# A gated conv and pooling trunk on eight cores: first-tile work in pieces, tanh gates, PSUM banks by last use

## The chip, the cores and the metric

One Trainium2 chip, all 8 cores. Each core runs the same program on one of the 8 prompt sequences and on 16 of the 128 sample sequences; the cores exchange nothing. The metric is the device time of the slowest core in microseconds.

## The reference

With `x` of 2048 tokens x 1024 channels (prompt) or 4 tokens x 1024 for each sample sequence, and six modulation vectors from `silu(c) @ w_ada + b_ada`:

```
h  = rms(x) * (1 + sc1) + sh1
z  = h @ w_in                       # a_val, a_gate, u, ga, gb, 1024 columns each
a  = a_val * sigmoid(a_gate)
cn = layernorm(depthwise_conv31(a) + conv_b)
o_a = silu(cn) @ w_conv_out
pooled = trailing_mean(u, window 2, 4, 8 or 16 by channel group) - u
o_b = (pooled @ pool_mix per group * pool_scale) @ w_pool_out
m  = sigmoid(ga) * o_a + sigmoid(gb) * o_b
x  = x + g1 * (m @ w_out)
x  = x + g2 * (relu(h2 @ w_ff1)^2 @ w_ff2)   # h2 = rms(x) * (1 + sc2) + sh2
y  = rms(x) * final_g
```

The last 30 rows of `a` and the last 15 of `u` are outputs too.

## The kernel before, in words

**Tiles.** Channels lie on the 128 partitions in 8 chunks `j`. The prompt is cut into 4 tiles of 512 tokens; the 64 sample tokens ride along with tile 0 (and with the MLP of tile 0) as extra matmuls of 64 columns. A stage is a loop over `j`: 8 matmuls 128x128x512 into one PSUM bank, then an eviction. The stages of a tile are A (the GLU, two groups a `j`), U (pooling input), G with index 0 and 1 (the two gates), PO and CO (the two branch outputs), O (output projection). The MLP, stage F, of tile t-1 stands between A and U of tile t.

**Weights.** They come in blocks of 1 MB of bf16 into 5 ring slots, in an order written out in `plan`. `use_block` takes the next block and issues loads up to 5 ahead (4 while a merge runs); each load goes into the slot that the block before has just left. A first load reads f32 and casts, from the POOL queue (L332); each block is saved once to a scratch in DRAM (L341, SP) and later read from there (L329, SP). In tile 0 the 12 blocks of `w_ada` stand between the others: `mod_half` (L491 on) turns one into half of a modulation vector. POOL runs its queue in order, so a load that waits for TensorE to leave a slot holds what is behind it.

**Tile 0.** All 31 conv taps run on TensorE as diagonal matrices (`conv0(p)`, two chunks a call, L738 on), with the sample's taps beside them (L717); diagonals are built two groups ahead by ScalarE (L697) and POOL (L700). `conv0` stands behind A `j` = 3, 5 and 7 and behind U `j` = 3. The sample history `shist` goes to `xT[1]` in one load (L1168), 8·16·34 bf16 elements a partition (1.1 MB), issued ahead of stage A; `pmT` and `uhist` (1344 f32 elements a partition, 0.69 MB) follow on SP (L1180, L1181). `s_pool` (L552 on) does the sample's pooling: 20 adds on POOL (L568) and 8 final operations on VectorE (L574). `merge_po` (L983 on) multiplies `pool_mix` into one half of `w_pool_out`: 8 chunks of 2 matmuls, evicted in turn by ScalarE (L993) and VectorE (L996), all in one piece ahead of PO `j` = 0 and 4.

**Later tiles.** 8 of the 31 taps run on TensorE, 23 on VectorE (L773), spread by a credit count (`pump`) over A, F, U and G0; `drain` finishes them ahead of `ln`.

**Small chains.** `rms_stats`, `s_rms` and `ln` sum squares by TensorE (L480, L526) into a PSUM bank, take a root on ScalarE, a reciprocal and a diagonal on VectorE (L465), and spread the result by a matmul with a matrix of ones (`bcast`, L474). They are generators; `hooks((j, step(g)), ...)` runs one step of `g` behind chunk `j` of a stage. `norm3` (final norm of the tile before, 8 VectorE operations at L671 that read its bank) stands in U, G0 `j` = 7 and G1 `j` = 0 to 2; `ln` (statistics, then 8 chunks by VectorE L809, POOL L811 and ScalarE Silu L813) in G1 `j` = 2, 6, 7 and PO 0 to 5; `norm1` of the next tile in PO, CO and O. ScalarE evicts gates with a Sigmoid (L971). VectorE multiplies them in at L1015 and L1035.

**PSUM.** `get_ps` hands out 4 general banks in turn, skipping held ones; `unhold`, at the point where the last reader is *issued*, puts a held bank back into the turn. The other 4 banks are for the conv.

```
i = rr["gen"]
while GEN[i] in held:
    i = (i + 1) % len(GEN)
rr["gen"] = (i + 1) % len(GEN)
```

Dependences are found by buffer (`Sched.op`): a reader waits for the last writer issued before it, a writer for the last writer and all readers. Each engine takes its instructions strictly in the order of the program.

## Time and profile before

| what | value |
|---|---|
| median of 3 runs | 1327.47 us (1325.97 to 1329.53) |
| the profiled execution, its own time | 1327.52 us |
| its span on the slowest core (core 0) | 1325.9 us |
| spans of the 8 cores | 1316.9 to 1325.9 us |
| mean granted TensorE clock by core | 0.940 to 0.943 |
| TensorE busy | 1138.7 us (86%) |
| VectorE, ScalarE, POOL busy | 50%, 41%, 35% |

How to read it: the span runs from the first instruction to the last on one core; 1.6 us of the time lie around it. Tile 0 takes the first 344 us (TensorE starts tile 1 at 344.1 us), three tiles with the MLP take about 270 us each, and the MLP of the last tile ends it. The granted clock is a share of 2.4 GHz; 0.5 is 1.2 GHz. A busy TensorE says nothing of its speed, so busy time and granted clock are read together.

### The profile page before, as it was taken

Reading aid. Unit: us, or ns where it says so; the run is one execution under the profiler, and the core shown is the slowest. Engines: PE = TensorE matmul, PEld = TensorE weight load, DVE = VectorE, ACT = ScalarE, POOL = GpSimd, SP = SyncE. Lnnn points to the kernel's source line nnn. Section 1 sums busy time; section 2 is a strip of 40 time slices with the busy share of each in tenths; the row PEclk is TensorE's granted clock in tenths of the full one; section 3 lists DMA queues with packets and bytes.
Section 4 is the critical chain, followed back from the end, with each engine's and each line's share of the span. In section 5 each row is a group of like instructions: output and inputs, shape, how many; then the busy total and the mean of one; then the engine's idle time right before and its main releaser. Section 6 shows DMA issues by size and latency. Waiting matters only on the chain.

```text
span 1325.9 us, 25435 instructions; the slowest of 8 cores (1316.9 to 1325.9 us)
## 1 busy us (share of the span) xinstructions
PE 1138.7 (86%) x6514; PEld 543.9 (41%) x6514; DVE 660.1 (50%) x1063; ACT 539.1 (41%) x970; POOL 469.0 (35%) x414
## 2 busy tenths in 40 slices
...
GB/s 170 211 166 65 101 71 170 188 95 221 162 136 141 166 146 172 151 221 193 128 164 190 155 191 227 164 213 131 124 195 174 186 181 127 162 128 96 159 96 64
DMA packets 40639, 205.52 MB, mean 155 GB/s; under 512 B 3968, under 2 KB 4352, under 8 KB 26496
## 3 DMA queue, kind: packets, MB, share of 16 engines
q0 software_dynamic: 20112, 76.62, 36.1%
q1 hardware_dynamic: 20384, 127.28, 28.3%
...
## 4 chain that ended last, share of the span: by engine, by line
PE 74%; DMA 6%; issue 5%; DVE 5%; ACT 4%; POOL 4%; POOLq 0%; DVEq 0%; SPq 0%; ACTq 0%
PE ps L383 47%; PE ps L1106 17%; PE ps L712 6%; DMA ring<-wblk 5%; PE ps L480 2%; PE ps L474 1%; POOL dgp L700 1%; DVE xT L671 1%; DMA xT<-xin 1%; POOL accN L447 1%; DVE tn L645 1%; POOL tn L811 1%; ACT tq L457 1%; POOL tp L888 1%; PE ps L717 1%
## 5 line engine op out<-in xcount | busy, mean ns | idle before, releaser
L773 DVE SCALAR_TENSOR_TENSOR ps<-aext,cw_sb,ps 128x512 f32<-128x512 bf16 x552 | 368.7, 749 | 5.2 <-PE ps L712 5.2
L383 PE MATMUL ps<-h,ring 128*128 128x512 bf16 x1280 | 303.7, 395 | 27.3 <-DMA ring<-wblk 22.7
L383 PE MATMUL ps<-s_t,ring 128*128 128x512 bf16 x1280 | 297.7, 389 | 14.1 <-ACT s_t L813 7.6
L1106 PE MATMUL ps<-r2f,ring 128*128 128x512 bf16 x1024 | 225.6, 382 | 5.1 <-ACT r2s L1095 5.1
L447 POOL TENSOR_TENSOR accN<-accN,tq 128x512 f32<-128x512 f32 x84 | 106.5, 1268 | 280.1 <-ACT tq L457 277.1
L383 PEld LDWEIGHTS ps<-h,ring 128*128 128x128 bf16 x1280 | 127.0, 102 | 184.9 <-issue 56.6
L383 PEld LDWEIGHTS ps<-s_t,ring 128*128 128x128 bf16 x1280 | 124.8, 100 | 168.3 <-issue 33.2
L332 POOL DMA_DIRECT2D ring<-wblk x72 | 52.9, 735 | 300.9 <-PE ps L383 178.8
L1106 PEld LDWEIGHTS ps<-r2f,ring 128*128 128x128 bf16 x1024 | 100.2, 98 | 125.9 <-issue 8.3
L457 ACT ACTIVATE tq<-xT 128x512 f32<-128x512 f32 x84 | 50.8, 624 | 215.8 <-DVE xT L1110 184.8
L383 PE MATMUL ps<-pooled,ring 128*128 128x512 bf16 x512 | 117.0, 383 | 11.6 <-DVE sgs L1044 4.1
L712 PE MATMUL ps<-aext,dgp 128*128 128x512 bf16 x440 | 109.1, 380 | 5.0 <-POOL dgp L700 5.0
L1082 ACT ACTIVATE ps<-ps 128x512 f32<-128x512 f32 x128 | 74.6, 583 | 92.5 <-PE ps L383 92.5
L1110 DVE SCALAR_TENSOR_TENSOR xT<-ps,modT,xT 128x512 f32<-128x512 f32 x32 | 24.0, 751 | 166.0 <-PE ps L1106 139.2
L700 POOL TENSOR_TENSOR dgp<-identb,cw_sb 128x1024 bf16<-128x1024 bf16 x36 | 67.8, 1893 | 85.9 <-PE ps L712 51.9
L1083 ACT ACTIVATE r2f<-ps 128x512 bf16<-128x512 f32 x128 | 76.4, 597 | 11.7
L383 PEld LDWEIGHTS ps<-pooled,ring 128*128 128x128 bf16 x512 | 48.8, 98 | 72.0 <-issue 17.7
L839 DVE TENSOR_TENSOR aext<-ps,tp 128x512 bf16<-128x512 f32 x32 | 22.1, 691 | 110.7 <-PE ps L383 96.3
L893 DVE SCALAR_TENSOR_TENSOR pooled<-tp,r2f 128x512 bf16<-128x512 f32 x32 | 36.2, 1138 | 77.3 <-POOL tp L888 48.0
L811 POOL TENSOR_TENSOR tn<-tn,bcs 128x512 f32<-128x512 f32 x32 | 40.1, 1265 | 85.1 <-DVE tn L809 85.1
L712 PEld LDWEIGHTS ps<-aext,dgp 128*128 128x128 bf16 x440 | 42.4, 97 | 59.0 <-issue 10.1
L971 ACT ACTIVATE r2f<-ps 128x512 f32<-128x512 f32 x64 | 36.6, 595 | 63.7 <-PE ps L383 59.8
...
## 6 DMA issues: line engine op xcount, KB each, us to landing
ring<-wblk POOLq DMA_DIRECT2D x72, 1024.0 KB, 11.1
ring<-wscr SPq DMA_DIRECT2D x68, 1024.0 KB, 6.3
wscr<-ring SPq DMA_DIRECT2D x32, 1024.0 KB, 9.8
xT<-xin SPq DMA_DIRECT2D x8, 1024.0 KB, 7.4
...
```

The source lines that it names most:

```text
L332: S.op("pool", lambda e: e.dma_start(out=ring[slot][:, :], in_=wblk[sid], max_dma_last_dim=8192), writes=[ringB[slot]], dma_key=("w", slot))
L383: S.op("pe", lambda e, l=l, r=r, i=i: e.matmul(ps[:, c0:c1], lhsT=l, rhs=r, start=(i == 0), stop=(i == n - 1)), reads=lB + rB, writes=[pB])
L447: S.op("pool", lambda e: e.tensor_tensor(out=acc[:, :], in0=i0, in1=ap, op=ALU.add), reads=[i0B, b, aBuf], writes=[aBuf])
L457: S.op("act", lambda e: e.activation(out=t_[:, 0:NT], in_=ap, func=AF.Square), reads=[b], writes=[tB_])
L700: S.op("pool", lambda e: e.tensor_tensor(out=dg[:, 0:n, :], in0=identb[:].unsqueeze(1).to_broadcast([128, n, 128]), in1=cw[:, j, k0:k0 + n ...
L712: S.op("pe", lambda e, k=k, dg=dg, k0=k0: e.matmul(ps[:, 0:NT], lhsT=dg[:, k - k0, :], rhs=aext[:, j, k:k + NT], start=(k == 0), stop=(k = ...
L773: S.op("dve", lambda e, j=j, k=k, ps=ps: e.scalar_tensor_tensor(out=ps[:, 0:NT], in0=aext[:, j, k:k + NT], scalar=cw[:, j, k:k + 1], in1=p ...
L811: S.op("pool", lambda e, t_=t_: e.tensor_tensor(out=t_[:, 0:NT], in0=t_[:, 0:NT], in1=bcs[:], op=ALU.add), reads=[tB_, bcsB], writes=[tB_])
L971: S.op("act", lambda e, ci=ci, pq=pq: e.activation(out=sg32[:, ci * 512:(ci + 1) * 512], in_=pq[:, 0:NT], func=AF.Sigmoid), reads=[pqB], w ...
L1082: S.op("act", lambda e, pf=pf: e.activation(out=pf[:, 0:NT], in_=pf[:, 0:NT], func=AF.Relu), reads=[pfB], writes=[pfB])
L1083: S.op("act", lambda e, j=j, pf=pf: e.activation(out=r2f[:, j * 512:(j + 1) * 512], in_=pf[:, 0:NT], func=AF.Square), reads=[pfB], writes= ...
L1106: S.op("pe", lambda e, k=k, pw=pw, slot=slot: e.matmul(pw[:, 0:NT], lhsT=slot[:, k * 128:(k + 1) * 128], rhs=r2f[:, k * 512:(k + 1) * 512] ...
```

## The change

- **PSUM banks.** `get_ps` gives the bank whose use was issued longest ago; `unhold` counts as a use.
- **Tile 0 order.** `conv0(j)` does one chunk. Calls stand behind A 3 (chunk 0), A 5 (1, 2), A 7 (3), U 3 (4), U 7 (5), G0 3 (6) and G0 7 (7). The `w_ada` blocks are spread in the same way, so none is left for G1.
- **Loads.** `shist` comes in four parts, two inside the first modulation work and two, with `uhist`, behind A `j` = 3. The load of `pmT` now names `aB[0]` as what it reads; the last writer of that at this point of the program is the memset of L410.
- **Merges.** `merge_po` is a generator of two chunks a step: the first half in G1 `j` = 3 to 6 of tile 0, the second in PO `j` = 0 to 3. Blocks marked `keep` stay in their slots until freed, and loads go no further than 5 past the oldest kept one.
- **Gates.** sigmoid(v) = (1 + tanh(v/2))/2: ScalarE writes tanh(v/2) (`AF.Tanh`, scale 0.5), VectorE computes (t + 1)·psum in one `scalar_tensor_tensor` for `tensor_tensor`, and the factor 1/2 goes into `g1` (one small VectorE operation in each of two `mod_half` calls). The Sigmoid of the GLU in stage A stays.
- **Chains.** `s_rms` yields between its Square and its sums. The sample layer norm `s_ln` moves from G0 (`j` = 0, 4) to G1 (0, 2), behind `s_pool`. In tile 0 `ln` stands in G1 3, 6, 7 and PO 0 to 5 (before: G1 1, 5, 6, 7 and PO 0 to 4). In tile 1's A the sample's norm starts at `j` = 0 and goes on at 3 and 5 (before: 3 and 5). In tiles 1 to 3 `norm3` stands in G1 `j` = 0 to 3, `ln` in G1 1, 4, 5, 6, 7 and PO 0 to 3; `norm1` is two to four chunks later in CO and O.

The diff, cut to its core (lines without their first eight spaces; `psv`, `step`, `hooks` unchanged; L1041's statements change like L1032's):

```diff
@@ -277,22 +277,25 @@
-rr = {"q": 0, "p": 0, "n": 0, "gen": 0, "stat": 0, "dg": 0, "dgb": 0}
+rr = {"q": 0, "p": 0, "n": 0, "stat": 0, "dg": 0, "dgb": 0}
...
+lru = list(GEN)
...
-    i = rr["gen"]
-    while GEN[i] in held:
-        i = (i + 1) % len(GEN)
-    rr["gen"] = (i + 1) % len(GEN)
+    i = next(b for b in lru if b not in held)
+    lru.remove(i)
+    lru.append(i)
...
-        held.add(GEN[i])
-    return psum[GEN[i]], psB[GEN[i]]
+        held.add(i)
+    return psum[i], psB[i]
...
-    held.discard(psB.index(psb))
+    i = psB.index(psb)
+    held.discard(i)
+    lru.remove(i)
+    lru.append(i)
@@ -342,14 +345,17 @@
-def use_block(want, hold_prev=False):
+kept = set()
...
+def use_block(want, keep=False):
...
-    depth = RING - 1 if hold_prev else RING
-    while blk["issued"] < min(bi + depth, len(plan)):
+    if keep:
+        kept.add(bi)
+    while blk["issued"] < min(min(kept | {bi}) + RING, len(plan)):
@@ -368,10 +374,9 @@
-plan += wseq(B_A, 3) + ada(G1, 0) + wseq(B_A + 3, 1) + ada(G1, 1) + wseq(B_U, 2) + ada(SC2, 0)
-plan += wseq(B_GA, 1) + ada(SC2, 1) + wseq(B_GA + 1, 1) + ada(SH2, 0) + wseq(B_GB, 1) + ada(SH2, 1) + wseq(B_GB + 1, 1)
-for b in range(2):
-    plan += [("raw", B_PO + b), ("merge", B_PO + b)]
+plan += wseq(B_A, 3) + ada(G1, 0) + wseq(B_A + 3, 1) + ada(G1, 1) + wseq(B_U, 1) + ada(SC2, 0) + wseq(B_U + 1, 1) + ada(SC2, 1)
+plan += wseq(B_GA, 1) + ada(SH2, 0) + wseq(B_GA + 1, 1) + ada(SH2, 1) + wseq(B_GB, 1)
+plan += [("raw", B_PO), ("merge", B_PO)] + wseq(B_GB + 1, 1) + [("raw", B_PO + 1), ("merge", B_PO + 1)]
@@ -500,6 +505,9 @@
+    if v == G1:
+        S.op("dve", lambda e: e.tensor_scalar(out=modT[:, c0:c0 + 4, :], in0=modT[:, c0:c0 + 4, :],
+                                              scalar1=0.5, scalar2=None, op0=ALU.mult), reads=[modB[v]], writes=[modB[v]])
@@ -521,6 +529,7 @@
+    yield
@@ -735,14 +744,13 @@
-def conv0(p):
-    if p == 0:
+def conv0(j):
+    if j == 0:
...
-    for j in (2 * p, 2 * p + 1):
-        bk = CVB[j % 3]
-        conv_taps_pe(0, j, psum[bk], psB[bk], CW, (psum[SCV], psB[SCV]))
-        conv_evict(j, psum[bk], psB[bk], *cstate["s"])
-    if p == 3:
+    bk = CVB[j % 3]
+    conv_taps_pe(0, j, psum[bk], psB[bk], CW, (psum[SCV], psB[SCV]))
+    conv_evict(j, psum[bk], psB[bk], *cstate["s"])
+    if j == NCH - 1:
@@ -968,7 +976,7 @@
-        S.op("act", lambda e, ci=ci, pq=pq: e.activation(out=sg32[:, ci * 512:(ci + 1) * 512], in_=pq[:, 0:NT], func=AF.Sigmoid),
+        S.op("act", lambda e, ci=ci, pq=pq: e.activation(out=sg32[:, ci * 512:(ci + 1) * 512], in_=pq[:, 0:NT], func=AF.Tanh, scale=0.5),
@@ -978,12 +986,13 @@
-        S.op("act", lambda e: e.activation(out=sgs[:, gi, :], in_=sp_[:, 0:512], func=AF.Sigmoid), reads=[spB], writes=[sgsB[gi]])
+        S.op("act", lambda e: e.activation(out=sgs[:, gi, :], in_=sp_[:, 0:512], func=AF.Tanh, scale=0.5), reads=[spB], writes=[sgsB[gi]])
...
-    src, srcB, _ = use_block(("raw", B_PO + b))
-    dst, dstB, bi = use_block(("merge", B_PO + b), hold_prev=True)
+    src, srcB, bsrc = use_block(("raw", B_PO + b), keep=True)
+    dst, dstB, bi = use_block(("merge", B_PO + b), keep=True)
+    merged[b] = (dst, [dstB] + mgB, bi)
@@ -995,8 +1004,13 @@
-    save_block(bi, B_PO + b, mgB)
-    return dst, [dstB] + mgB
+        if c == NCH - 1:
+            kept.discard(bsrc)
+            save_block(bi, B_PO + b, mgB)
+        if c % 2 == 1:
+            yield
...
+merged = {}
@@ -1005,21 +1019,23 @@
-                slot, slL = merge_po(j // 4)
+                slot, slL, bmerged = merged[j // 4]
...
-        S.op("dve", lambda e, pb_=pb_, sgb=sgb: e.tensor_tensor(out=sgb, in0=pb_[:, 0:NT], in1=sgb, op=ALU.mult),
+        S.op("dve", lambda e, pb_=pb_, sgb=sgb: e.scalar_tensor_tensor(out=sgb, in0=sgb, scalar=1.0, in1=pb_[:, 0:NT], op0=ALU.add, op1=ALU.mult),
...
+            if j % 4 == 3:
+                kept.discard(bmerged)
...
-        S.op("dve", lambda e: e.tensor_tensor(out=sgs[:, 1, :], in0=sp_[:, 0:512], in1=sgs[:, 1, :], op=ALU.mult),
+        S.op("dve", lambda e: e.scalar_tensor_tensor(out=sgs[:, 1, :], in0=sgs[:, 1, :], scalar=1.0, in1=sp_[:, 0:512], op0=ALU.add, op1=ALU.mult),
@@ -1032,7 +1048,7 @@
-        S.op("dve", lambda e, pa_=pa_, sga=sga: e.tensor_tensor(out=sga, in0=pa_[:, 0:NT], in1=sga, op=ALU.mult),
+        S.op("dve", lambda e, pa_=pa_, sga=sga: e.scalar_tensor_tensor(out=sga, in0=sga, scalar=1.0, in1=pa_[:, 0:NT], op0=ALU.add, op1=ALU.mult),
@@ -1165,20 +1181,33 @@
-S.op("pool", lambda e: e.dma_start(out=aes.rearrange("p c n w -> p (c n w)"), in_=shist, max_dma_last_dim=8192),
-     writes=aesB, dma_key=("c", 8))
+AWC = 2 * NS * AWS
...
+def load_sh(p):
+    S.op("pool", lambda e: e.dma_start(out=aes[:, 2 * p:2 * p + 2, :, :].rearrange("p c n w -> p (c n w)"),
+                                       in_=shist[:, p * AWC:(p + 1) * AWC], max_dma_last_dim=8192),
+         writes=[aesB[p]], dma_key=("sh", p))
...
-for v in (SC1, SH1):
-    mod_half(v, 0)
-    mod_half(v, 1)
+next(sn0)
+mod_half(SC1, 0)
+load_sh(0)
+mod_half(SC1, 1)
+mod_half(SH1, 0)
+load_sh(1)
+mod_half(SH1, 1)
...
-S.op("sp", lambda e: e.dma_start(out=pmF, in_=pmT_in), reads=[modB[SC1]], writes=plB, dma_key=("c", 6))
-S.op("sp", lambda e: e.dma_start(out=uxs[:, 0:UTOT], in_=uhist), reads=[modB[SH1]], writes=sB + uxsB, dma_key=("c", 7))
+S.op("sp", lambda e: e.dma_start(out=pmF, in_=pmT_in), reads=[aB[0]], writes=plB, dma_key=("c", 6))
...
+def late_loads():
+    load_sh(2)
+    load_sh(3)
+    S.op("sp", lambda e: e.dma_start(out=uxs[:, 0:UTOT], in_=uhist), reads=[aB[3]], writes=sB + uxsB, dma_key=("c", 7))
@@ -1187,49 +1216,56 @@
-def cv(p):
-    return lambda: conv0(p)
...
-stage_A(0, hooks((3, cv(0)), (5, pm_scale), (5, lambda: mod_half(G1, 0)), (5, cv(1)), (7, lambda: mod_half(G1, 1)), (7, cv(2))))
-chains = stage_U(0, hooks((3, cv(3)), (7, lambda: mod_half(SC2, 0))))
+def cv(*js):
+    def go():
+        for j in js:
+            conv0(j)
+    return go
...
+def md(v, b):
+    return lambda: mod_half(v, b)
...
+stage_A(0, hooks((3, late_loads), (3, cv(0)), (5, md(G1, 0)), (5, cv(1, 2)), (7, md(G1, 1)), (7, pm_scale), (7, cv(3))))
+chains = stage_U(0, hooks((3, md(SC2, 0)), (3, cv(4)), (7, md(SC2, 1)), (7, cv(5))))
...
+stage_G(0, 0, hooks((3, md(SH2, 0)), (3, cv(6)), (7, md(SH2, 1)), (7, cv(7))), chains)
+s_pool()
...
-stage_G(0, 0, hooks((0, step(lns)), (4, step(lns)), (3, lambda: mod_half(SC2, 1)), (7, lambda: mod_half(SH2, 0))), chains)
-s_pool()
-stage_G(0, 1, hooks((1, step(lnp)), (3, lambda: mod_half(SH2, 1)), *[(j, step(lnp)) for j in (5, 6, 7)]))
+mg0, mg1 = merge_po(0), merge_po(1)
+stage_G(0, 1, hooks((0, step(lns)), (2, step(lns)), (3, step(lnp)), *[(j, step(mg0)) for j in (3, 4, 5, 6)], (6, step(lnp)), (7, step(lnp))))
...
-stage_PO(0, hooks(*[(j, step(lnp)) for j in range(5)], *[(j, step(n1)) for j in (1, 3, 5, 7)]))
-stage_CO(0, hooks((1, step(n1)), (5, step(n1)), (7, step(n1))))
-stage_O(0, hooks((0, step(n1)), (2, step(n1))))
+stage_PO(0, hooks(*[(j, step(mg1)) for j in range(4)], *[(j, step(lnp)) for j in range(6)], *[(j, step(n1)) for j in (1, 3, 5, 7)]))
+stage_CO(0, hooks((3, step(n1)), (7, step(n1))))
+stage_O(0, hooks((1, step(n1)), (3, step(n1)), (5, step(n1))))
...
-        acts += [(3, step(sn2)), (5, step(sn2))]
+        acts += [(0, step(sn2)), (3, step(sn2)), (5, step(sn2))]
...
-        acts += [(4, step(sf)), (7, step(sf))]
+        acts += [(3, step(sf)), (4, step(sf)), (7, step(sf))]
...
-    stage_G(t, 0, hooks((7, step(n3))), chains)
+    stage_G(t, 0, hooks(), chains)
...
-    acts = [(0, step(n3)), (1, step(n3)), (2, step(n3)), (2, step(lnp)), (6, step(lnp)), (7, step(lnp))]
+    acts = [(0, step(n3)), (1, step(lnp)), (1, step(n3)), (2, step(n3)), (3, step(n3))] + [(j, step(lnp)) for j in (4, 5, 6, 7)]
...
-        acts.append((3, lambda t=t: load_x(t + 1)))
+        acts.append((4, lambda t=t: load_x(t + 1)))
...
-    stage_PO(t, hooks(*[(j, step(lnp)) for j in range(6)], *[(j, step(n1)) for j in (1, 3, 5, 7)]))
-    stage_CO(t, hooks((1, step(n1)), (5, step(n1)), (7, step(n1))))
-    stage_O(t, hooks((0, step(n1)), (2, step(n1))))
+    stage_PO(t, hooks(*[(j, step(lnp)) for j in range(4)], *[(j, step(n1)) for j in (1, 3, 5, 7)]))
+    stage_CO(t, hooks((3, step(n1)), (7, step(n1))))
+    stage_O(t, hooks((1, step(n1)), (3, step(n1)), (5, step(n1))))
```

## Rows read from the trace of the kernel before

**Rows 1.** The profile's page, whole run: engines, DMA queues, one costly group, block loads.

```profile
PE 1138.7 (86%) x6514; PEld 543.9 (41%) x6514; DVE 660.1 (50%) x1063; ACT 539.1 (41%) x970; POOL 469.0 (35%) x414
...
q0 software_dynamic: 20112, 76.62, 36.1%
q1 hardware_dynamic: 20384, 127.28, 28.3%
...
L383 PE MATMUL ps<-h,ring 128*128 128x512 bf16 x1280 | 303.7, 395 | 27.3 <-DMA ring<-wblk 22.7
...
ring<-wblk POOLq DMA_DIRECT2D x72, 1024.0 KB, 11.1
```

**Rows 2.** Busy time by stretch; last columns granted clock, DMA share, GB/s.

```profile
100.00:190.00 90.00, 85.61 (x761) 45.88 (x760) 13.33 (x26) 59.16 (x171) 54.77 (x44) 1.00 0.41 70
190.00:345.00 155.00, 106.09 (x802) 52.01 (x802) 54.25 (x98) 56.02 (x78) 57.63 (x66) 0.85 0.86 177
580.00:590.00 10.00, 6.33 (x23) 4.45 (x24) 4.03 (x9) 1.75 (x3) 0.00 (x0) 0.56 0.85 264
```

**Rows 3.** Who TensorE waited for, 60 to 345 us (total, times, longest).

```profile
PE ps L383 <- DMA ring<-wblk: 28.2, 3, 14.2
PE ps L383 <- ACT ring L993: 9.8, 3, 6.0
PE ps L383 <- ACT r2f L971: 6.5, 3, 3.4
...
PE ps L383 <- DVE sgs L1044: 4.1, 1, 4.1
PE ps L383 <- DVE stat L792: 2.9, 1, 2.9
```

**Rows 4.** TensorE in order of time (start, length, idle before), tile 0.

```profile
72.55 5.29 PE L383 MATMUL ps<-h,ring 128*128 128x512 bf16 x16 [7.70 <-DMA ring<-wblk]
...
227.43 3.15 PE L383 MATMUL ps<-h,ring 128*128 128x512 bf16 x7 [6.25 <-DMA ring<-wblk]
```

**Rows 5.** All engines in order of time, 230 to 244 us.

```profile
231.61 1.29 POOL L568 TENSOR_TENSOR tp<-s_t 128x288 f32<-128x288 f32 x2
...
239.10 1.22 DVE L574 SCALAR_TENSOR_TENSOR pls<-tp,s_t 128x64 bf16<-128x64 f32 x4 [0.63 <-POOL tp L568]
...
240.26 0.16 DVE L787 TENSOR_TENSOR stat<-ps,stat 128x4 f32<-128x4 f32 x1
...
242.74 1.29 DVE L465 TENSOR_TENSOR dgb<-ident,stat 128x512 f32<-128x512 f32 x2
```

**Rows 6.** Who TensorE waited for, 345 us to the end.

```profile
PE ps L480 <- DVE xT L671: 19.3, 3, 7.6
PE ps L480 <- POOL accN L447: 12.7, 4, 3.5
PE ps L383 <- ACT s_t L813: 7.6, 4, 3.3
PE ps L526 <- ACT tq L522: 7.6, 2, 5.6
PE ps L1106 <- ACT r2s L1095: 5.1, 1, 5.1
...
PE ps L383 <- ACT r2s L1095: 4.3, 2, 2.5
PE ps L383 <- ACT r2f L971: 4.0, 3, 1.3
```

**Rows 7.** All engines in order of time, 826 to 872 us (tile 2).

```profile
844.04 1.26 POOL L447 TENSOR_TENSOR acc<-acc,tq 128x512 f32<-128x512 f32 x1
...
848.73 5.34 DVE L671 SCALAR_TENSOR_TENSOR xT<-xT,vecs,ps 128x512 f32<-128x512 f32 x8
...
854.22 3.55 PE L480 MATMUL ps<-oned,acc 128*128 128x1 f32 x16 [7.62 <-DVE xT L671]
```

**Rows 8.** ScalarE in order of time, 250 to 270 us.

```profile
257.69 1.28 ACT L813 ACT_TABLE_LOAD   x1
```

More of the change, by code:

```diff
@@ L542, in s_norm @@
         def s_norm(dst, dstB, vsc, vsh):
-            d, dB = s_rms()
+            d, dB = yield from s_rms()
             yield
```

2 lines of the change are left out of this document (1 added, 1 removed).

## The prediction

> **What bounds the kernel now.** I read the page first. TensorE is busy 86% of the span and no other engine over 50% [rows 1], so the question is where TensorE waits and where it runs slowly. The busy time by stretch comes second: from 100 to 190 us TensorE works 85.6 of 90 us at full clock while the DMA engines are 41% busy; from 190 to 345 us it works 106 of 155 us at a mean clock of 0.85 and the DMA engines are 86% busy [rows 2]. Tile 0 thus has a stretch where the loads idle and one where they are late. Third, TensorE's waits. In tile 0: 28.2 us for blocks of weights, then 9.8, 6.5, 4.1 and 2.9 us around the merges, the layer norm and the end of CO [rows 3]; the order of time adds that the 28.2 us are 7.7 ending at 72.6 us and two waits in G, the longest of 14.2 [rows 3] and one of 6.3 ending at 227.4 us [rows 4], 20.5 together. Behind tile 0: 19.3 us for VectorE's L671, three times, and some 40 us in smaller items [rows 6].
>
> A wait costs more than its length. In the 10 us around the end of the L671 wait of tile 1 the granted clock is 0.56, the lower level of 1.2 GHz for most of it, with 6.3 us of work [rows 2]: 2.8 us lost, and some more behind it. After the wait ending at 227 us 7 matmuls took 3.15 us [rows 4], where the whole group averages 303.7/1280 = 0.24 us each, so 1.7 us. I price the slow work behind a wait of some 4 us or more at 3 to 3.5 us.
>
> **Tile 0, what goes.**
> (a) Second block of A. Ahead of it in the queues stand the whole `shist` and `uhist`. The cast loads took 36.1% of 1325.9 us for 76.62 MB, 6.2 us a MB; the other queue 28.3% for 127.28 MB, 2.9 us a MB [rows 1]. Three quarters of 1.1 MB are 5.2 us, 0.69 MB are 2.0 us: A's second block starts 7.2 us earlier. `pmT` moves to the very start, since its new condition is a memset long done; its bytes stay ahead of A, so it gives nothing and costs nothing.
> (b) The 20.5 us for blocks in G. Conv chunks and `w_ada` blocks now alternate with the weight blocks, so loads are asked for evenly. Demand from 100 to 345 us was 0.41·90 + 0.86·155 = 170 us of DMA time [rows 2]; compressed into some 200 us it is 85%, tight, but it fits. 20.5 us go.
> (c) 9.8 + 6.5 + 4.1 + 2.9 = 23.3 us of waits. The merges stood bare: TensorE made two matmuls and waited for evictions; now they stand between gate chunks. The 6.5 us are ScalarE alternating Sigmoid and Silu with a 1.28 us table load each time [rows 8]. The 4.1 us before O are a bank just handed back by CO's sample sum: last in the turn now.
> (d) Slow clock behind four of these waits, 3 us each: 12 us (bound: 15% of 106 us, 16).
> Sum 63 us.
>
> **Tile 0, what comes.**
> (e) `s_ln` is now behind `s_pool`. On VectorE its first operation (L787) stands behind the last L574, and that behind POOL's 20 adds, which began at 231.6 us; the last L574 ran from 239.1, L787 at 240.3, and the diagonal followed 2.5 us later [rows 5]. With the last conv chunk ending at T, POOL first has two evictions' adds of 1.26 us [rows 7] behind ScalarE's, so it reaches `s_pool` at about T + 3.8 and ends it at T + 12; the diagonal is there at T + 15. TensorE has three gate chunks (each 8·0.24 plus 8 small ones, 2.2 us) and 16 tiny matmuls till the step at `j` = 2: T + 8. A wait of 7 us plus 3 of slow clock: 10 us, between 3 (POOL nearly done) and 14.
> (f) ScalarE's root waits for L787 too, with the gates behind it; it catches up over two chunks: 2 us.
> (g) CO. `ln` now goes on to PO `j` = 5, as in tiles 1 and 2 before, where CO's start waited 3.7 us each (7.6 in all) [rows 6]. And since merged blocks are kept, CO's second block is asked for only at CO's start, behind POOL's last adds (up to 4 us); it lands 11.1 us on [rows 1], needed after four chunks, 9 us. Together 6, with clock 9 us; between 3 and 14.
> (h) O's first chunk waits 2 us for its input instead of its bank.
> Sum 23 us; tile 0 gives 63 - 23 = 40 us.
>
> **Tiles 1 to 3.**
> (i) The bank. In tile 2 the last sum that `ln` needs was added by 845.3 us, but its matmul started at 854.2, when the eighth L671 was through (848.7 + 5.3) [rows 7]: it had been given the bank that `norm3` was still reading. By last use this bank comes last. That frees 19.3 us, the 4.0 us for the gate eviction between table loads [rows 6] and 3·3.5 of clock: 34 us. What is late next: VectorE still has to get through `norm3`'s first two (0.67 us each) before the statistics, ScalarE's root holds two gates up, and with one bank held TensorE comes back to `norm3`'s bank at `j` = 5 while the last L671 run: 3 us a tile. Net 25 us; between 10 and 34.
> (j) CO's start. With `ln` at G1 4 to 7 and PO 0 to 3 its last chunk is ready about 3.5 us or more before CO: the 7.6 us go. `norm1`'s sum moves from CO 1 to CO 3, past POOL's last adds: two of the four waits of L480, say 6.0 of 12.7 us [rows 6]. Clock twice 3. 19.6 us; the other two waits (last tile) stay.
> (k) Tile 1's sample work. L526 waited 5.6 and 2.0 us for a Square in ScalarE's queue; it is now issued a step ahead, but the next chunk then waits for the bank `norm2` reads, an estimated 2.2 us (its eight reads of some 0.67 us start four chunks earlier): 5.4 us go. The waits for L1095, 5.1 + 4.3 us, were for a bank just handed back: gone. Clock 4. 18.8 us.
> Sum 63 us.
>
> **Costed at nothing.** `scalar_tensor_tensor` for `tensor_tensor` (64 evictions) and the small halving of `g1`: VectorE is 50% busy [rows 1] and four banks stand between it and TensorE; if that cover is gone each costs its lengthening, well under 0.1 us. Extra issues for `shist` on POOL (three more): under a microsecond each, while POOL waits anyway. Two conv diagonals in a row on ScalarE for chunks 6 and 7: now with G0 between them. More waits of POOL's loads, one behind each `w_ada` block, hold the next diagonal back, but the diagonals are two groups ahead. The start and the last tile's MLP are not touched.
>
> **Sum.** 40 + 63 = 103 us off the profiled execution's 1327.5 us (span 1325.9 and 1.6 around it), which is the median's time too: 1224.5, said as 1225 us.
>
> **Table loads.** The sum takes it that Tanh and Silu need no reload between them. No row shows a Tanh, so it is bounded: all reloads between gates and Silu gone, or all kept. If kept, each of the four `ln` chunks now inside G1 pairs a gate and a Silu with two loads: 2·1.28 [rows 8] + 1.4 = 4.0 us of ScalarE against 1.9 of TensorE, 8 us behind per tile. I take the first, since Square, Copy and Identity run between Silus with no load, so sets hold several functions.
>
> The Trainium skill (ScalarE: Activation LUTs, section Table sets) names Tanh in the sets of exp and of sigmoid and names no set with Silu; by that list the gates and Silu would still reload, which is rival 1. Its section on what a load costs gives about 2.66 us a switch with a drain, twice the 1.28 us of the trace's load; by the page's figure the kept case would be some 50 us dear instead of 28, so the time would be near 1275.
>
> **Rivals.**
> 1. *Reloads stay* (above): 4·(4.0 - 1.9) = 8 us a tile in tiles 1 to 3, half in tile 0, less what banks cover, and the 4.0 + 6.5 us of waits kept partly: about 28 us, 1253. Chance 0.10.
> 2. *Tile 0 stays bound by its loads.* For it: 86% DMA from 190 us on, and 85% demand when compressed; all eight cores read at once. Against it: 41% for 90 us. Waits of (b) come back further on: 1225 + 28 = 1253. Chance 0.14.
> 3. *The new waits do not come* ((e), (g) and the 9 of (i) mostly hidden by slack in order): 1225 - 28 = 1197. Chance 0.13.
> 4. *Slower than before.* TensorE's clock. It is granted 0.94 on the mean; were the denser stream granted less, the whole stream would stretch. With about 1090 us of matmul time left of 1138.7 [rows 1] and a clock I expect at 0.96, the gain of 103 us is eaten at 9.4% more, that is below a mean clock of 0.88; at 0.86 the time is 1225 + 1090·(0.96/0.86 - 1), about 1352. Against it: 85.6 busy of 90 us at 1.00 [rows 2]. Chance 0.04.
> 5. The bank order does nothing (the wait at `ln` was for the sums, not the bank): 24 us of (i) stay, 1250. Against it the 9 us between the last add and the matmul [rows 7]. Chance 0.04.
>
> **Numbers.** Forecast 0.55. The range 1195 to 1262 takes rivals 1, 2, 3 and 5 and the open ends of (e), (g), (i); left out are rival 4 and pairs of misses. About 0.3% (4 us) is what can be told from no change: faster 0.94, same 0.02, slower 0.04.
>
> **What would show it.** Right: no wait for blocks from 90 to 200 us, TensorE starting tile 1 near 304 us; a wait of 5 to 10 us for a diagonal in the third chunk of G1 of tile 0, ended by VectorE's L465 behind L574; no wait of the `ln` sums for L671; few table loads at the gates; mean clock 0.96. Wrong: waits for `ring` in G or CO of tile 0, a table load at each gate of G1, or a granted clock under 0.9.

## The result, and the profile after

The changed kernel takes 1274.8 us (median of 4 runs, 1272.4 to 1275.4) against 1327.2 us before: a ratio of 0.96, 95% interval 0.9581 to 0.9618. I had said 1225 us, range 1195 to 1262. The direction was right and the size about half; the time lies outside the range. Lines of the changed kernel are 5 to 16 higher: L383 is L388 there, L447 L452, L480 L485, L671 L680, L700 (a conv diagonal on POOL) L709, L712 (conv taps) L721, L813 L821, L971 L979, L993 L1002, L1044 L1060. In some executions part of the cores were granted a lower clock than the rest, whatever the kernel: the medians below leave these executions out, and where a kernel has hardly any others, its cores at the higher clock are compared.

First the page of the profile after, rows that answer to [rows 1]:

```profile
PE 1122.4 (88%) x6514; PEld 539.5 (42%) x6514; DVE 665.7 (52%) x1065; ACT 516.3 (41%) x952; POOL 471.6 (37%) x417
...
L388 PE MATMUL ps<-s_t,ring 128*128 128x512 bf16 x1280 | 294.1, 386 | 22.7 <-DMA ring<-wblk 12.6
...
ring<-wblk POOLq DMA_DIRECT2D x72, 1024.0 KB, 12.6
```

TensorE has the same 6514 matmuls in 16 us less, since more of them ran at the upper clock (cores 0.955 to 0.962 on the mean, 0.940 to 0.943 before). ScalarE has 952 instructions where it had 970: 18 table loads fewer.

TensorE's waits behind tile 0, after (answers to [rows 6]):

```profile
PE ps L485 <- POOL accN L452: 10.9, 4, 3.4
PE ps L388 <- ACT s_t L821: 5.4, 2, 4.7
PE ps L388 <- DVE xT L680: 5.2, 3, 1.7
...
PE ps L535 <- ACT tq L530: 0.6, 1, 0.6
```

The 19.3 us for L671 at L480 are gone. What is left of that tile (L680) is three waits of at most 1.7 us: TensorE coming back to `norm3`'s bank, which step (i) had named. The sample's 7.6 us are 0.6, and the L1095 waits are off the list. So behind tile 0 the planned waits went, but for L485 <- L452: 10.9 us in four waits, where half of 12.7 was to go.

TensorE's waits in tile 0, after (answers to [rows 3]):

```profile
PE ps L721 <- POOL dgp L709: 17.6, 7, 12.6
PE ps L388 <- DMA ring<-wblk: 12.6, 1, 12.6
PE ps L593 <- DVE cfs L755: 11.3, 1, 11.3
PE ps L388 <- ACT ring L1002: 6.2, 2, 5.2
PE ps L545 <- DVE dgb L470: 2.9, 1, 2.9
PE ps L388 <- ACT r2f L979: 2.3, 2, 1.9
```

Three single waits of these (12.6, 12.6 and 11.3) take 36.5 us together, and none of them stood at these places before. The other cores have them too: on the six of the eight that I read the first is 12.6 us, the block 9.9 to 13.8 and L755 9.0 to 12.8. The stretches (columns as in [rows 2]: length, busy time by engine, granted clock, DMA share, GB/s):

```profile
100.00:190.00 90.00, 73.14 (x655) 38.67 (x653) 18.23 (x36) 46.77 (x132) 48.65 (x41) 0.91 0.71 119
190.00:345.00 155.00, 114.38 (x786) 58.46 (x784) 49.80 (x85) 52.80 (x98) 59.14 (x65) 0.82 0.62 138
140.00:150.00 10.00, 1.59 (x7) 0.74 (x8) 0.75 (x2) 0.00 (x0) 4.24 (x4) 0.50 0.20 33
310.00:320.00 10.00, 3.12 (x8) 1.17 (x9) 0.00 (x0) 0.00 (x0) 3.94 (x4) 0.50 1.03 158
```

The loads are evenly spread, as meant: 0.41 and 0.86 of the DMA engines became 0.71 and 0.62. But the stretch that ran at 85.6 of 90 us and clock 1.00 now has 73.1 us at 0.91, and around each long wait the clock is at its lower level. TensorE in order of time shows where tile 0 ends:

```profile
62.74 3.61 PE L388 MATMUL ps<-h,ring 128*128 128x512 bf16 x16
...
148.41 0.58 PE L721 MATMUL ps<-aext,dgp 128*128 128x512 bf16 x1 [12.62 <-POOL dgp L709]
...
222.47 1.84 PE L593 MATMUL ps<-oned,cfs 128*64 128x1 f32 x16 [11.32 <-DVE cfs L755]
...
280.48 3.57 PE L388 MATMUL ps<-pooled,ring 128*128 128x512 bf16 x8 [5.17 <-ACT ring L1002]
...
316.88 3.40 PE L388 MATMUL ps<-s_t,ring 128*128 128x512 bf16 x8 [12.57 <-DMA ring<-wblk]
...
344.44 3.62 PE L388 MATMUL ps<-h,ring 128*128 128x512 bf16 x16
```

A's second block starts at 62.7 us without a wait (72.6 before, [rows 4]; 2.5 of these 9.8 us are A's own earlier start), but tile 1 starts at 344.4 us, and before it started at 344.1. Tile 0 gave nothing; all 53 us come from behind it. The question for the experiments is therefore where tile 0's 40 us went.

**The three waits, traced back.** POOL in order of time before the first:

```profile
128.00 1.07 POOL L896 TENSOR_TENSOR tp<-r2f 128x526 f32<-128x526 f32 x1
...
139.34 2.43 POOL L896 TENSOR_TENSOR tp<-tp 128x524 f32<-128x524 f32 x2 [0.26 <-POOL tp L896]
145.36 0.74 POOL L335 DMA_DIRECT2D ring<-wblk  x1 [3.60 <-issue]
146.38 1.88 POOL L709 TENSOR_TENSOR dgp<-identb,cw_sb 128x1024 bf16<-128x1024 bf16 x1 [0.28 <-issue]
```

Chunk 4's diagonal is built on POOL, and chunk 4 now stands in U, where POOL also runs the pooling adds (L896): 14 us of them, then a block load, then the diagonal. Only chunks 6 and 7 build all diagonals on ScalarE, and in the kernel before those were the two that stood in U. The 3.6 us of "issue" ahead of the load are semaphore waits, as `one_wait_per_semaphore` below shows: the scheduler emits one for each reader of the buffer, 64 matmuls here, 0.06 us each.

The second wait begins with the state copies. DMA issues from 176 to 215 us, with the time from issue to landing in the last column:

```profile
ring<-wblk POOLq DMA_DIRECT2D x2, 1024.0 KB, 18.8
ncs_old<-sconv SPq DMA_DIRECT2D x1, 1664.0 KB, 15.7
wscr<-ring SPq DMA_DIRECT2D x1, 1024.0 KB, 26.4
nps_old<-spool SPq DMA_DIRECT2D x1, 704.0 KB, 21.3
```

The save of G0's block (L344) is issued right behind the two copies and takes 26.4 us to land, where the same save takes 5.3 with the copies moved (`copies_late`). POOL's next load overwrites that slot and so stands in POOL's queue until 211.1 us, which is the save's landing at 206.4 and the semaphore waits; the convolution's and pooling's adds are behind it, VectorE waits for those, and the sample's conv eviction (L755), for which TensorE waits, is behind them on VectorE. The profile puts POOL's idle time down to TensorE's L388, whose last matmul ended at 211.1 us too; in `one_wait_per_semaphore` the save lands at 199.6 and the load starts at 200.3 us.

The kernel before has the same two copies ahead of the same save, but there TensorE waited for something else. Its two block waits in G end with loads that POOL had issued at 191.1 and 193.5 us, while the copies ran, and that were 29 and 34 us under way. The second load, from the chain that ended last, and the first wait:

```profile
193.50 33.69 DMA ring<-wblk
...
220.18 1.00 PE L383 MATMUL ps<-scT,ring 128*128 128x17 bf16 x32 [14.24 <-DMA ring<-wblk]
```

So the copies do two things: loads beside them land late, and a save behind them holds POOL.

The third: CO's second block is asked for at 306.15 us, since `keep` holds the ring until CO, and is needed from 304 us on.

### The profile page after: what moved, and what is told of

It reads as the page before. It is cut to its first block, busy times and chain, and to the rows that moved or that the text cites. A ratio compares the mean times of both kernels' runs of the same rounds, so it can differ in the third digit from the quotient of the medians.

```text
span 1273.0 us, 25253 instructions; the slowest of 8 cores (1258.3 to 1273.0 us)
## 1 busy us (share of the span) xinstructions
PE 1122.4 (88%) x6514; PEld 539.5 (42%) x6514; DVE 665.7 (52%) x1065; ACT 516.3 (41%) x952; POOL 471.6 (37%) x417
## 4 chain that ended last, share of the span: by engine, by line
PE 79%; DMA 7%; DVE 5%; issue 4%; POOL 3%; ACT 2%; POOLq 0%; DVEq 0%; ACTq 0%; SPq 0%
PE ps L388 51%; PE ps L1122 17%; PE ps L721 7%; DMA ring<-wblk 5%; PE ps L485 2%; DMA xT<-xin 1%; DVE tn L654 1%; POOL dgp L709 1%; PE ps L479 1%; DVE xT L680 1%; POOL accN L452 1%; DMA yo<-xT 1%; POOL tp L896 1%; PE ps L726 1%; POOL tn L819 1%
## 5 line engine op out<-in xcount | busy, mean ns | idle before, releaser
L388 PE MATMUL ps<-h,ring 128*128 128x512 bf16 x1280 | 297.3, 388 | 22.5 <-DVE stat L800 6.3
L388 PE MATMUL ps<-s_t,ring 128*128 128x512 bf16 x1280 | 294.1, 386 | 22.7 <-DMA ring<-wblk 12.6
L452 POOL TENSOR_TENSOR accN<-accN,tq 128x512 f32<-128x512 f32 x84 | 106.7, 1270 | 279.2 <-ACT tq L462 274.1
L388 PEld LDWEIGHTS ps<-h,ring 128*128 128x128 bf16 x1280 | 124.3, 100 | 177.6 <-issue 44.9
L388 PEld LDWEIGHTS ps<-s_t,ring 128*128 128x128 bf16 x1280 | 124.2, 99 | 174.0 <-issue 37.1
L721 PE MATMUL ps<-aext,dgp 128*128 128x512 bf16 x440 | 112.3, 389 | 17.6 <-POOL dgp L709 17.6
L388 PE MATMUL ps<-pooled,ring 128*128 128x512 bf16 x512 | 115.9, 383 | 9.3 <-ACT ring L1002 6.2
L709 POOL TENSOR_TENSOR dgp<-identb,cw_sb 128x1024 bf16<-128x1024 bf16 x36 | 68.1, 1902 | 71.5 <-PE ps L721 50.5
L388 PEld LDWEIGHTS ps<-pooled,ring 128*128 128x128 bf16 x512 | 49.3, 98 | 70.6 <-issue 15.6
L721 PEld LDWEIGHTS ps<-aext,dgp 128*128 128x128 bf16 x440 | 43.2, 99 | 72.8 <-issue 24.5
L706 ACT ACTIVATE dgp<-identb,cw_sb 128x128 bf16<-128x128 bf16 x152 | 47.1, 390 | 40.5 <-PE ps L726 40.1
L896 POOL TENSOR_TENSOR tp<-tp 128x524 f32<-128x524 f32 (+2 forms) x48 | 58.8, 1225 | 9.0 <-POOL tp L896 2.9
## 6 DMA issues: line engine op xcount, KB each, us to landing
ring<-wblk POOLq DMA_DIRECT2D x72, 1024.0 KB, 12.6
```

What stands on the lines that cost most here:

```text
L388: S.op("pe", lambda e, l=l, r=r, i=i: e.matmul(ps[:, c0:c1], lhsT=l, rhs=r, start=(i == 0), stop=(i == n - 1)), reads=lB + rB, writes=[pB])
L452: S.op("pool", lambda e: e.tensor_tensor(out=acc[:, :], in0=i0, in1=ap, op=ALU.add), reads=[i0B, b, aBuf], writes=[aBuf])
L709: S.op("pool", lambda e: e.tensor_tensor(out=dg[:, 0:n, :], in0=identb[:].unsqueeze(1).to_broadcast([128, n, 128]), in1=cw[:, j, k0:k0 + n ...
L721: S.op("pe", lambda e, k=k, dg=dg, k0=k0: e.matmul(ps[:, 0:NT], lhsT=dg[:, k - k0, :], rhs=aext[:, j, k:k + NT], start=(k == 0), stop=(k = ...
L896: S.op("pool", lambda e, prev=prev, nx=nx, lo=lo, d=d: e.tensor_tensor(out=nx[:, lo:UW], in0=prev[:, lo:UW], in1=prev[:, lo - d:UW - d], o ...
```

## The experiments

Each comes with runs of the kernel before on the same chip, and the ratio is to those. The changed kernel itself was not run again beside them; that its 1274.8 us may be compared rests on the kernel before, whose cores at the higher clock had 1312 to 1326 us on every occasion. Tile 1's start and the rest of the span, on the slowest core of each profile, split every result in two; four more kernels stand in the text alone:

| kernel | median us | ratio, 95% | tile 1 starts | rest |
|---|---|---|---|---|
| before | 1327.2 | | 344.1 | 981.8 |
| changed | 1274.8 | 0.9581–0.9618 | 344.4 | 928.6 |
| banks only | 1295.3 | 0.9700–0.9838 | 337.7 | 955.5 |
| tanh only | 1314.6 | 0.9883–0.9939 | 334.2 | 978.9 |
| all but tile 0's order | 1269.9 | 0.9513–0.9620 | 330.1 | 939.1 |
| changed, diagonals on ScalarE | 1256.9 | 0.9405–0.9531 | 330.6 | 925.4 |
| changed, state copies later | 1259.6 | 0.9412–0.9552 | 332.8 | 922.5 |
| changed, earlier refill | 1267.0 | 0.9468–0.9607 | 338.5 | 927.0 |
| changed, one wait per semaphore | 1249.8 | 0.9364–0.9471 | 322.2 | 925.5 |
| changed, all four | 1230.2 | 0.9131–0.9244 | 301.3 | 927.3 |

The slowest core is one of eight whose spans differ by 8 to 24 us, so a part of a few us read from this table is rough. Where it matters the median over the eight cores is given beside it; for the changed kernel this is a span of 1263.5 us (1321.7 before), tile 1 at 341.4 us (342.0 before) and a rest of 922.7 (979.1 before).

### Which part gave what

**`banks_only`**

```diff
-            i = rr["gen"]
-            while GEN[i] in held:
-                i = (i + 1) % len(GEN)
-            rr["gen"] = (i + 1) % len(GEN)
+            i = next(b for b in lru if b not in held)
+            lru.remove(i)
+            lru.append(i)
...
```

and `unhold` likewise puts its bank last.

> The kernel before with get_ps and unhold as in the changed kernel (banks by last use), nothing else. My step (i): the 19.3 us of TensorE's waits for VectorE's L671 in tiles 1 to 3 go, with some of the clock behind them, less what is late next: 10 to 30 us faster, about 20. Since the gates are still Sigmoid next to Silu, the 4 us for the gate eviction may stay. The 4.1 us before O in tile 0 (the bank just handed back) and some of the 5.1 + 4.3 us for L1095 go too: 3 to 8 us more. Together 15 to 35 us, near 1300. Rival 5 (the wait was for the sums and not the bank): less than 5 us, and a wait of the same length at L480 ended by POOL or ScalarE instead.

Measured: 1295.3 us, 30 less than its own runs of before (1325.8); 26.3 of them behind tile 0 (29 on the median core). TensorE's waits behind tile 0:

```profile
PE ps L386 <- ACT s_t L816: 18.6, 6, 8.7
```

No wait for `xT` is left at the `ln` sums, so the wait was for the bank: rival 5 is refuted. But what is late next is larger than I said. CO's start now waits up to 8.7 us for `ln`'s last Silu, 18.6 us in all where it was 7.6 [rows 6]: part of the wait had only moved.

**`tanh_only`**

```diff
-  e.activation(out=sg32[...], in_=pq[:, 0:NT], func=AF.Sigmoid)
+  e.activation(out=sg32[...], in_=pq[:, 0:NT], func=AF.Tanh, scale=0.5)
```

with the halved `g1`, the sample's gates and the four evictions that add one.

> The kernel before with the gates as tanh of half the argument (L971 and its sample twin, the halved g1, the four evictions with plus one), nothing else. Theory: Tanh and Silu need no table load between them, so the loads at the layer norm's Silu go (instructions of ScalarE fall from 970 to about 950), and with them the waits for the gates' eviction: 6.5 us in tile 0 and 4.0 us behind it, with some clock: 5 to 12 us faster. The L671 waits in tiles 1 to 3 stay. Rival (the reloads weren't on the path, other waits hide them): under 3 us, though the loads go. Rival 1 of the prediction (reloads stay) would show the same count of loads and no gain.

Measured: 1314.6 us, 11 less, as expected, 9.9 of them in tile 0. ScalarE has 952 instructions as in the changed kernel. The wait for the gate's eviction in tile 0 fell from 6.5 us [rows 3] to 1.4, while L671's stayed:

```profile
PE ps L480 <- DVE xT L674: 19.3, 3, 7.6
...
PE ps L383 <- ACT r2f L974: 1.4, 2, 0.7
```

Rival 1 is refuted. ScalarE of the changed kernel in the middle of `ln` shows why, Silu (L821), Tanh (L979), Silu with no load between:

```profile
262.56 0.82 ACT L821 ACTIVATE s_t<-tn,vecs 128x512 bf16<-128x512 f32 x1 [2.58 <-POOL tn L819]
263.28 0.58 ACT L979 ACTIVATE r2f<-ps 128x512 f32<-128x512 f32 x1
263.78 0.82 ACT L821 ACTIVATE s_t<-tn,vecs 128x512 bf16<-128x512 f32 x1
```

The Trainium skill (ScalarE: Activation LUTs, Table sets) names no set that has Silu; here the trace differs from what its list suggested, and the trace decides. That the changed kernel's 1274.8 us meet the 1275 of the prediction's dearest case, loads kept at twice the price, is chance: the loads went.

**`steady_part`**: the kernel before with banks, tanh and the new places in tiles 1 to 3, but tile 0 in its old order.

```diff
-            stage_G(t, 0, hooks((7, step(n3))), chains)
+            stage_G(t, 0, hooks(), chains)
...
-            acts = [(0, step(n3)), (1, step(n3)), (2, step(n3)), (2, step(lnp)), (6, step(lnp)), (7, step(lnp))]
+            acts = [(0, step(n3)), (1, step(lnp)), (1, step(n3)), (2, step(n3)), (3, step(n3))] + [(j, step(lnp)) for j in (4, 5, 6, 7)]
```

> The kernel before with all that the change does outside tile 0: banks by last use, tanh gates, and the new places of norm3, ln, load_x and norm1 in tiles 1 to 3; tile 0 keeps its order (but has the banks and the tanh). Theory: tiles 1 to 3 give about 57 us as they did in the changed kernel, and tile 0 gains from banks and tanh alone some 5 to 12 us, since its own order loses as much as it gains: 1255 to 1268, so as fast as the changed kernel or faster by up to 15 us. Rival (tile 0's new order carries a gain that its new waits only partly eat): 1285 or slower, that is clearly slower than the changed kernel.

Measured: 1269.9 us, just over the range expected and no slower than the changed kernel. Behind tile 0 it gave 42.7 us (47.5 on the median core), not 57. Its waits behind tile 0:

```profile
PE ps L386 <- ACT s_t L819: 8.7, 2, 8.1
PE ps L532 <- ACT tq L528: 7.6, 2, 5.6
```

CO's 18.6 us are 8.7 now, since `ln` stands inside the second gate: behind tile 0 the banks give 26.3 us, tanh 2.9, and by difference the places 13.5 (29, 2 and 17 on the median core). The changed kernel gains another 10.5 there (9 on the median core). Of what it has and this kernel lacks, the sample steps of tile 1 act there, and the 7.6 us of L528 are 0.6 in it; the steps were not run by themselves. In tile 0 banks and tanh gave 14.0 us, yet in the changed kernel tile 0 gives nothing: its new order as written costs 14 us.

### What tile 0's new order ran into

**`diag_on_act`**

```diff
-            if t == 0 and (g % 2 == 1 or j >= 6):
+            if t == 0 and (g % 2 == 1 or j >= 4):
```

> The changed kernel with the diagonals of conv chunks 4 and 5 built by ScalarE alone, as those of 6 and 7 are. Theory (POOL's queue): chunk 4 now stands in U, and its POOL diagonal waits behind 11 pooling adds and a block load, 12.6 us. Taking POOL out of it removes that wait and the 2.5 us one of chunk 5, with 3 to 4 us of slow clock behind them: 13 to 18 us less than the changed kernel's 1275, so about 1259. Rival (tile 0 is bound by its loads): the time comes back as waits for ring blocks or further on, under 5 us gained. Second rival (ScalarE too slow: 31 diagonals take 9.4 us against 8.6 of matmuls): small waits for ScalarE, 2 to 6 us, so about 1264.

Measured: 1256.9 us, 18 less than the changed kernel (15 on the median core). Waits in tile 0:

```profile
PE ps L388 <- DMA ring<-wblk: 22.5, 3, 13.5
...
PE ps L721 <- POOL dgp L709: 2.5, 5, 1.6
```

17.6 us for the diagonals are 2.5. A block wait of 7.5 us, ending at 186.7 us, comes in their place: its load was issued at 156.9 us and was 29.6 us under way beside the state copies. In the changed kernel the same load, issued at 166.6 us, had landed in 10.0 before the copies began at 178.6. So part of the block waits was gone there only because the diagonal was late. Tile 1 starts 13.8 us earlier.

**`copies_late`**: the two copies `ncs_old`, `nps_old` behind tile 0.

```diff
-        S.op("sp", lambda e: e.dma_start(out=ncs_old, ...), dma_key=("o", 5), out_dma=True)
-        S.op("sp", lambda e: e.dma_start(out=nps_old, ...), dma_key=("o", 6), out_dma=True)
         stage_G(0, 0, ...)
...
         stage_O(0, ...)
+        S.op("sp", lambda e: e.dma_start(out=ncs_old, ...), dma_key=("o", 5), out_dma=True)
+        S.op("sp", lambda e: e.dma_start(out=nps_old, ...), dma_key=("o", 6), out_dma=True)
```

> The changed kernel with the two copies of old sample state (DRAM to DRAM, 2.3 MB) issued after tile 0's O instead of after U. Theory: POOL stood 20 us (186 to 206 us) on the save of a ring block that these copies hold up, and with it the conv adds, VectorE and the sample's layer norm (TensorE wait of 11.3 us for L755). Without them this wait goes to under 1 us, the diagonal wait behind s_pool grows from 2.9 to about 7 us as the prediction had it, net 7 to 11 us less: about 1266. Rival (the wait belongs to POOL's own work and waits for readers): under 3 us gained.

Measured: 1259.6 us, 15 less (11 on the median core), more than expected. The 11.3 us for L755 are gone and the sample's diagonal is late instead:

```profile
PE ps L545 <- DVE dgb L470: 7.8, 1, 7.8
```

7.8 us is the wait that step (e) had put at 7. It had been hidden behind the larger one.

**`before_copies_late`**: the same move in the kernel before.

> The kernel before with the same two copies moved behind tile 0's O. The prediction laid the 20.5 us of block waits in G to the order of conv chunks and modulation blocks. Theory now: they are the two copies, which share the DMA engines from 188 to 213 us. Then the waits of 14.2 and 6.3 us fall below 5 us in all and the time by 15 to 24 us, to about 1307. If the prediction's cause was right: under 5 us gained, 1322 or more.

Measured, in six executions and on the cores at a clock of 0.94 or more: 1299 to 1308 us, against 1314 to 1325 for such cores of before. On core 5 of the profile the waits for blocks in tile 0:

```profile
PE ps L383 <- DMA ring<-wblk: 13.0, 2, 9.4
```

of which 9.4 is A's second block; in G one of 3.6 is left of 20.5. So 17 of the 20.5 us of (b) were not for the order of the loads: they were for the copies' traffic beside two loads. I had read who TensorE waited for, and not that these loads, issued at 191.1 and 193.5 us, were about three times as long under way as the median block load (11.1 us, [rows 1]), nor what ran beside them.

**`refill_early`**

```diff
                     if j % 4 == 3:
                         kept.discard(bmerged)
+                        refill()
```

where `refill()` issues what fits in the ring.

> The changed kernel with loads issued again as soon as a kept block is freed (PO chunks 3 and 7) and not only at CO's start. Theory: CO's second block was late (wait of 12.6 us on the slowest core) only because it was asked for at CO's start behind POOL's queue. The wait goes; the layer norm's chunk that it hid may show 3 to 4 us: net 9 to 14 us less, about 1264. Rival (the DMA engines are full there): the block still lands late, under 4 us gained.

Measured: 1267.0 us, 8 less, but only some 2 on the median core: under what was expected, and the rival's "under 4 us" is not excluded. The wait for CO's block went, and another came at the start of O:

```profile
PE ps L394 <- POOL pooled L1060: 10.3, 2, 9.7
```

The next load of the ring now stands on POOL between CO's fourth add and its last two (L1060): POOL stood 13.1 us at it, to 318.8, with the adds behind. POOL's queue carries both, and one or the other is late.

**`one_wait_per_semaphore`**: ahead of an instruction, only the highest value of each semaphore is waited for.

```diff
+                    last = {}
                     for d in ins.deps:
                         key, sem, val = signal_of(d)
+                        if key not in last or last[key][2] < val:
+                            last[key] = (key, sem, val)
+                    for key, sem, val in last.values():
```

> The changed kernel with one semaphore wait per semaphore ahead of an instruction (the highest value) where it had one for every reader; the order of all work is the same. Theory: 64 waits of 0.06 us stand ahead of each block load on POOL's queue, about 4 us each, and 13 us of them on SP's before load_x. Without them POOL reaches the diagonal of chunk 4 about 4 us sooner, so the 12.6 us wait at 148 us shrinks to 8 or 9, the 11.3 us wait for the conv sample eviction shrinks by about 4, and CO's second block lands up to 4 us sooner: 5 to 15 us faster than the changed kernel. Rival (the waits lie beside the load's own wait, and POOL would have stood anyway): under 3 us.

Measured: 1249.8 us, 25 less (21 on the median core), more than expected. POOL at the diagonal of chunk 4:

```profile
139.52 2.49 POOL L900 TENSOR_TENSOR tp<-tp 128x524 f32<-128x524 f32 x2 [0.20 <-POOL tp L900]
141.95 0.74 POOL L339 DMA_DIRECT2D ring<-wblk  x1
142.71 1.91 POOL L713 TENSOR_TENSOR dgp<-identb,cw_sb 128x1024 bf16<-128x1024 bf16 x1
```

The load follows the last add at once, and chunk 4 waits 8.7 us instead of 12.6. That puts TensorE 3.7 us ahead there, and it is 5.5 ahead at the end of the wait for L755, though that wait grew to 13.6 us where it was expected to shrink. Up to PO's start (264.0 us, here 250.9) it gains 7.6 more: the 2.9 us for the sample's diagonal are gone, and from 230 to 280 us the clock is 0.97 where it was 0.81. The next 6.4 us, up to CO's start, are mostly SyncE's queue. In the program `load_x(1)` has 248 semaphore waits ahead of it; the two loads of x, in the changed kernel and in this one:

```profile
272.79 6.22 SPq L622 DMA_DIRECT2D xT<-xin  x2
```

```profile
246.60 9.71 SPq L626 DMA_DIRECT2D xT<-xin  x2
```

In the changed kernel ScalarE has `norm1`'s first copy of x in its queue ahead of a merge's eviction (L1002), and so TensorE waits 5.2 us at 280.5 us for a load that it does not need until tile 1. That wait is 1.0 us here. The last 3 us come at CO's second block, whose wait is 9.4 us for 12.6.

**`before_one_wait`**: the same edit in the kernel before.

> The kernel before with one wait per semaphore. In the changed kernel this gave 24 us, twice what the 4 us a block on POOL's queue explain. Theory A: the gain is tile 0's alone, where POOL both asks for blocks and works; the kernel before has the same queue and gains 8 to 20 us, nearly all of it before 350 us. Theory B: the many waits cost in every tile (SyncE's queue ahead of the loads of weights and of x, VectorE's too): then the time from the start of tile 1 to the end shortens as well, by 5 us or more. Theory C: it only helps where the diagonals are late, as in the changed kernel: under 5 us here.

Measured: a ratio of 0.9719 to 1.0031 to its runs of before, which tells little. In the profiled execution all cores have a clock of 0.94 or more: 1316.7 us against 1327.5 for that of before; tile 1 starts at 336.7 (7.4 earlier), and the rest is 978.2 (3.6 less). Theory A as to place, at the low end as to size. The changed kernel gains over twice as much from the same edit, and there POOL and SyncE sit on TensorE's path.

**`tile0_four_fixes`**: the four edits together.

> The changed kernel with all four edits that gained alone: diagonals of chunks 4 and 5 on ScalarE (18 us), state copies behind tile 0 (14 us), CO's second block asked for as soon as PO's merged block is free (6.6 us), one wait per semaphore (24 us). They share two waits (the diagonal of chunk 4, the conv sample eviction), so not all of 62 us: theory 35 to 50 us below the changed kernel, 1225 to 1240, with tile 1 starting near 310 us. Rival (the loads of tile 0 are then the bound, rival 2 of the prediction): a wait for blocks of weights of 10 us or more in G comes and the time stays over 1240.

Measured: 1230.2 us (1230.1 to 1232.1), 45 less than the changed kernel (39 on the median core). Tile 1 starts at 301.3 us. Waits in tile 0 (core 4):

```profile
PE ps L398 <- POOL pooled L1064: 8.7, 2, 8.1
PE ps L555 <- DVE dgb L480: 6.4, 1, 6.4
...
PE ps L398 <- DMA ring<-wblk: 1.9, 1, 1.9
```

The 8.1 us at O's start are POOL's, and its row names the save of a block's slot, 18.7 us under way, as what it waited for:

```profile
282.09 0.74 POOL L339 DMA_DIRECT2D ring<-wblk  x1 [11.53 <-DMA wscr<-ring]
282.85 2.49 POOL L1064 TENSOR_TENSOR pooled<-r2f 128x512 bf16<-128x512 f32 x2
```

Waits for blocks are down to 1.9 us at a DMA share of 0.82 from 60 to 345 us. Rival 2, that tile 0 stays bound by its loads, is refuted for the part behind 60 us. Ahead of that it stands: TensorE works 15 of 60 us in the kernel before and 20 here, with the DMA engines at 0.98 and 0.99.

**`tile0_five_fixes`**: and `s_pool` behind `s_ln`'s second step.

```diff
-        s_pool()
         lns, lnp = s_ln(), ln(0)
...
-        stage_G(0, 1, hooks((0, step(lns)), (2, step(lns)), (3, step(lnp)), ...
+        stage_G(0, 1, hooks((0, step(lns)), (2, step(lns)), (2, s_pool), (3, step(lnp)), ...
```

> As the kernel with four edits, and s_pool put behind s_ln's second step in the second gate instead of ahead of it. My step (e) said that s_pool ahead of s_ln costs 7 us of wait for the diagonal and 3 of slow clock; the kernel with late copies showed 7.8 us of wait. Theory: that wait goes: 5 to 10 us below the kernel with four edits. Rival: ln's own diagonals and the merges then stand behind the pooling adds on POOL and VectorE and wait the same: within 3 us.

Measured: 1228.0 us against 1230.2, in the one execution of five whose cores all have a clock of 0.96 or more, so the rival is nearer than the theory. On core 5 of the profile the sample's diagonal waits 0.6 us instead of 6.4, but the statistics of `ln` then wait:

```profile
PE ps L398 <- DVE stat L810: 4.5, 1, 4.5
```

The eight cores of that execution have a median of 1219.3 us, where those of the kernel with four edits have 1222.5 to 1225.2: a gain of 2 to 6 us is left.

**`steady_plus_fixes`**: tile 0 in its old order, with the change's other parts, late copies and one wait per semaphore.

> The kernel before's order of tile 0 with the change's other parts (banks, tanh, places in tiles 1 to 3, the sample steps a step earlier), late state copies and one wait per semaphore. It tells whether the new order of tile 0 is worth keeping at all. From 1269.9 us of the steady part: sample steps 9 us, copies 14 to 18, waits 8 to 20: 1225 to 1240. If the new order is worth something once its own waits are gone, this kernel is slower than the one with four or five edits by over 5 us; if not, it is as fast.

Measured: 1254.1 us, with some cores at a clock of 0.95 in every run and others at 0.97; the latter have 1224.8 to 1239.6 us, where the profile of the kernel with four edits has 1214.4 to 1228.6. Core 0 starts tile 1 at 309.0 us. Once its obstacles are gone, the new order of tile 0 is worth some 9 us over the old one (medians of these cores 1233.8 and 1225.2), and not the 40 of the prediction.

## Why the prediction was wrong, step by step

**Costed at nothing: the diagonals.** POOL's loads "hold the next diagonal back, but the diagonals are two groups ahead". This is the step that failed most. I had looked at chunks 6 and 7, which moved out of U, and not at 4 and 5, which moved in. They cost two waits, 12.6 us at 148.4 and 2.5 for chunk 5, and the clock fell from 1.00 to 0.91 for the stretch. Undone, they gave 18 us.

**(b) The block waits, 20.5 us.** I laid them to the order of the loads; moving the two state copies alone took 17 us of them away. In the changed kernel no wait for a block is left in G, but the copies stayed: they came back as 11.3 us for `cfs`, and as a block wait of 7.5 us once the diagonal's wait was gone. A wait whose cause was misread had been booked as a gain.

**(e) and (f), `s_ln`.** Size right, as the 7.8 us under late copies show; in the changed kernel it was 2.9 us behind the 11.3 us of (b).

**(g) CO's second block.** I put 6 us on CO's start and its second block together, since the request would stand behind "POOL's last adds (up to 4 us)". POOL reached it at 306.2 us, 11.3 after CO had begun and not 4, and TensorE waited 12.6. It is `norm1`'s adds that POOL had first, and 3.1 us of semaphore waits.

**(c) and (d).** Of 23.3 us of waits around the merges, some 10 stay: L1002 6.2, L979 2.3 and 1.4 for the sample's last add (L1062). Step (c) looked at ScalarE's tables and not at `norm1` in the same queue. The 12 us of clock could not come while there were four waits as long as the old ones.

**(a)** was right and small: the wait of 7.7 us is gone, 7.2 was forecast.

**(i) to (k).** 63 us forecast, 53 measured behind tile 0. Banks alone gave 26.3 there (29 on the median core). I had 25 for `ln` and the 9.4 of L1095, 34 together, but the bank freed at `ln` left CO's start late, which only (j)'s new places repaired. (j) is by difference 13.5 for 19.6, or 17 on the median core; its waits for POOL's L452 stayed, 10.9 us where 6.7 were to be left. (k)'s sample step is at most 10.5, for 5.4 and its share of the clock. Tanh's 2.9 close the sum.

With four obstacles removed tile 1 starts at 301.3 us, where I had said 304, and the time is 1230.2. That is near the forecast by luck. Two of the four edits, the late copies and the single waits, stand in no step of the prediction and help the old order as well: with them it starts tile 1 at 309.0 us. Banks and tanh bring tile 1 from 344.1 to 330.1 us, these two edits on to 309.0, and the new order, to which the prediction gave most of the 40 us, the last 8. The prediction summed what each wait would give back and never replayed POOL's queue in U with chunk 4 in it.
